# The input projections of the second block as three float32r products of split operands

## The reference

```python
u = rms_norm(h, w_norm_mix[l])
proj = jnp.einsum('btd,dk->btk', u, w_in[l])
conf_a = proj[..., OFF_CONF:OFF_CONF + CONF_WIDTH]
conf_g = proj[..., OFF_CONF + CONF_WIDTH:OFF_Z]
z = proj[..., OFF_Z:OFF_XBC]
xbc = proj[..., OFF_XBC:OFF_DT]
dt_raw = proj[..., OFF_DT:OFF_GATE]
gates = jax.nn.sigmoid(proj[..., OFF_GATE:].astype(jnp.float32)).astype(h.dtype)

c = conf_a * jax.nn.sigmoid(conf_g)
c = depthwise_conv(c, w_conf_dw[l], b_conf_dw[l])
xbc = jax.nn.silu(depthwise_conv(xbc, w_ssm_conv[l], b_ssm_conv[l]))
y = bidir_ssd(xs, dt_raw, ssm_dt_bias[l], ssm_a_log[l], Bs, Cs, ssm_d[l]).reshape(b, Lt, SSM_INNER)
y = rms_norm(y * jax.nn.silu(z), w_ssm_norm[l])
```

## Time and profile before

| what | value |
|---|---|
| median of 3 runs | 2759.58 us |
| lowest, highest | 2759.31, 2762.41 us |
| profiled execution | 2761.74 us |
| its span in the trace | 2760.0 us |
| mean granted TensorE clock | 0.976 |
| scan and what follows it up to the tail | 733 to 1465 us |
| of it the groups 0 to 3 | 797 to 1388 us |
| experts (L1067) | from 1698 us to the end |

### The profile page before, as it was taken

The page is one execution under the profiler, slowest core; times in us unless marked ns, Lnnn a source line. Parts: engine busy times, 40 slices in busy tenths (PEclk is TensorE's granted clock), DMA queues, the critical chain, the costliest instruction groups (busy, mean ns, idle before and its releaser), DMA issues.

```text
span 2760.0 us, 39931 instructions
## 1 busy us (share of the span) xinstructions
PE 2640.1 (96%) x17315; PEld 1608.2 (58%) x17315; DVE 1012.5 (37%) x1458; ACT 673.3 (24%) x1198; POOL 215.7 (8%) x218
## 2 busy tenths in 40 slices
PE   8998899999999999999879997999999999999996
PEld 6754478888787877878669993333333333333332
DVE  4335444433346868685835423111111111111111
ACT  3255433222223333332344222000000000000001
POOL 0022000000002112121200000000000000000000
PEclk9999999999999999999989999999999999999998
DMA  5100022222314142323322246999999999999993
GB/s 203 69 23 1 31 92 92 106 80 97 119 41 140 54 132 62 121 50 92 87 109 82 86 200 244 404 400 407 399 404 394 401 394 398 398 394 391 398 400 135
DMA packets 92619, 560.78 MB, mean 203 GB/s; under 512 B 15236, under 2 KB 48004, under 8 KB 59812
## 3 DMA queue, kind: packets, MB, share of 16 engines
q1 hardware_dynamic: 40320, 514.89, 47.2%
q10 hardware_dynamic: 47236, 30.42, 4.0%
q0 software_dynamic: 4896, 12.98, 1.8%
HBM read 541.97 MB, written 16.29 MB: 202 GB/s over the span
## 4 chain that ended last, share of the span: by engine, by line
PE 90%; DVE 7%; issue 1%; ACT 1%; DMA 0%; POOL 0%; POOLq 0%; ACTq 0%; DVEq 0%; SPq 0%
PE PS L1067 36%; PE PS L509 17%; PE PS L969 5%; PE PS L732 4%; PE PS L728 4%; PE PS L729 4%; PE PS L974 2%; PE PS L703 2%; PE PS L636 2%; DVE H L1878 1%; PE PS L583 1%; PE PS L584 1%; PE PS L587 1%; PE PS L522 1%; PE PS L1057 1%
## 5 line engine op out<-in xcount | busy, mean ns | idle before, releaser
L509 PE MATMUL PS<-U,ring 128*128 128x264 f32 x2304 | 527.4, 389 | 1.3 <-ACT arena L1360 1.3
L1067 PE MATMUL PS<-expert_ring_low,U 128*32 128x512 f32 x4608 | 509.9, 594 | 0.9 <-DVE U L2095 0.9
L1067 PE MATMUL PS<-expert_ring_high,U 128*32 128x512 f32 x4608 | 504.8, 593 | 0.0
L509 PEld LDWEIGHTS PS<-U,ring 128*128 128x128 f32 x2304 | 436.7, 191 | 80.6 <-issue 8.5
L1067 PEld LDWEIGHTS PS<-expert_ring_high,U 128*32 128x32 f32 x4608 | 148.3, 110 | 336.6 <-issue 335.6
L1067 PEld LDWEIGHTS PS<-expert_ring_low,U 128*32 128x32 f32 x4608 | 146.6, 110 | 332.6 <-issue 331.5
L1878 DVE SCALAR_TENSOR_TENSOR H<-arena,par,H 128x528 f32<-128x528 f32 x240 | 188.5, 829 | 1.4
L2107 DVE TENSOR_TENSOR H<-H,PS 128x512 f32<-128x512 f32 x32 | 22.0, 688 | 439.8 <-PE PS L1067 424.3
L728 PE MATMUL PS<-UX,WF 128*128 128x512 f32 x352 | 138.0, 392 | 0.8 <-DVE UX L1639 0.8
L729 PE MATMUL PS<-UX,WF 128*128 128x512 f32 x352 | 137.1, 390 | 0.0
L1290 ACT ACTIVATE WF<-ring 128x1024 fp32r<-128x1024 f32 (+1 forms) x76 | 72.0, 948 | 246.2 <-PE PS L732 245.6
(11 more groups left out here) (327 smaller groups left out, 3214.1 us busy)
## 6 DMA issues: line engine op xcount, KB each, us to landing
expert_ring_low<-w_experts SPq DMA_DIRECT2D x96, 2048.0 KB, 11.3
expert_ring_high<-w_experts SPq DMA_DIRECT2D x96, 2048.0 KB, 11.2
ring<-w_gu SPq DMA_DIRECT2D x11, 2048.0 KB, 7.8
ring<-ssd_sums ACTq DMA_DIRECT2D x32, 512.0 KB, 7.5
ring<-w_xbc SPq DMA_DIRECT2D x8, 1536.0 KB, 6.5
ring<-w_down SPq DMA_DIRECT2D x8, 1408.0 KB, 5.9
ring<-w_in SPq DMA_DIRECT2D x5, 2048.0 KB, 7.9
ring<-w_conf SPq DMA_DIRECT2D x8, 1024.0 KB, 8.6
```

The lines of the kernel that those rows point to most:

```text
L509: last = nc.tensor.matmul(PS[0:M, banks[i], 0:hi - lo], lhs(k), rhs(k)[:, lo:hi], start=(k == 0), stop=(k == K - 1))
L1067: mm = nc.tensor.matmul(PS[QUAD * t:QUAD * t + QUAD, bank, :], stat(t), move(t), start=start, stop=stop)
```

## The change

Each of the 73 projections becomes three float32r products of split operands, as in the tail: weights high x U high, weights high x U low, weights low x U high, 48 matmuls of 264 columns in place of 16 in float32. U is split once, after the normalisation: ScalarE writes the rounded tiles into free space of the ring, VectorE the remainders into `UH`.

Weights now come tile by tile (`w_scan`, 512 KB each) in the order in which PE uses them (`SCAN`), through four places. A tile's load waits until PE has ended the tile four earlier. ScalarE rounds a tile into one of three buffers; it does so directly behind the evacuation of the tile three earlier (`piece_taken`). VectorE subtracts in place (`scan_lows`), at places written into its list. PE waits for the rounded tile ahead of a projection (`fw_high`) and for the remainder ahead of its last 16 matmuls (`fw_low`). The decay arrays move to a slot of their own. The four tail copies into `WH` move behind the last gate tiles on ScalarE, and the loads of `w_co` wait for the last gate tile.

```diff
+SCAN = [("dt",), ("xb", 0, 0), ("xb", 0, 1)] + [(part, u) for u in range(CONF_AHEAD) for part in ("ca", "cg")]
+CHUNK_LAST = {}
+
+
+def _gates(at):
+    SCAN.extend(tag for tag, place in zip(GATE_OF, GATES_AT) if place == at)
+
+
+for _g in range(GROUPS):
+    SCAN += [("xb", _g, _t) for _t in range(6) if _t >= 2 or (_g > 0 and _t == 1)]
+    _gates((_g, "conv"))
+    SCAN += [("zt", 4 * _g), ("zt", 4 * _g + 1)]
+    _gates((_g, "late"))
+    SCAN += [("zt", 4 * _g + 2), ("zt", 4 * _g + 3)]
+    for _c in range(5):
+        _gates((_g, _c))
+        if _g < GROUPS - 1:
+            SCAN.append(("xb", _g + 1, 0) if _c == 4 else (("ca", "cg")[_c % 2], 2 * _g + CONF_AHEAD + _c // 2))
+        CHUNK_LAST[_g, _c] = len(SCAN) - 1
+SCAN += [("g1", m) for m in range(4, DT)]
+SCAN_AT = {tag: n for n, tag in enumerate(SCAN)}
+SRAW, SHIGH = 4, 3
...
+        def scan_place(of, n):
+
+            slot_, at = (RING - 1, max(0, PIECE * n - 512)) if n < SRAW else (0, PIECE * (n % SRAW))
+            width = 64 if n == 0 else P
+            return of[:, slot_, at:at + DT * width].rearrange("p (k n) -> p k n", k=DT)
+
+        def scan_split(n):
+            width = 64 if n == 0 else P
+            at = PIECE * (n % SHIGH)
+            return RF[:, 1, at:at + DT * width].rearrange("p (k n) -> p k n", k=DT)
+
+        def u_high(k):
+            return RF[:, 2, k * T2:k * T2 + T2] if k < DT - 1 else RF[:, 1, PIECE * SHIGH:PIECE * SHIGH + T2]
...
+            def scan_dense(tag, banks, M=P, first=False):
+
+                n = SCAN_AT[tag]
+                open_(tag, *banks)
+                wh, wl = scan_split(n), scan_place(RF, n)
+                pe.wait_ge(S("fw_high"), len(pieces) + n + 1)
+                for k in range(DT):
+                    if first:
+                        pe.wait_ge(S("ux_low"), 2 * DT + k + 1)
+                    for part, x in enumerate((u_high(k), UH[:, k, :])):
+                        for i, (lo, hi) in enumerate(halves(T2)):
+                            nc.tensor.matmul(PS[0:M, banks[i], 0:HT], wh[:, k, :], x[:, lo:hi], start=(k == 0 and part == 0), stop=False)
+                pe.wait_ge(S("fw_low"), len(pieces) + n + 1)
+                for k in range(DT):
+                    for i, (lo, hi) in enumerate(halves(T2)):
+                        last = nc.tensor.matmul(PS[0:M, banks[i], 0:HT], wl[:, k, :], u_high(k)[:, lo:hi], start=False, stop=(k == DT - 1))
+                fill(last, tag)
+
+            scan_dense(("dt",), (6, 7), M=64, first=True)
...
-                dense(tag, (b, b + 1), DT, T2, lambda k: w[:, k, cols], lambda k: U[:, k, :], reads=name)
+                scan_dense(tag, (b, b + 1))
...
+            def scan_highs(upto):
+
+                while scan_next[0] <= min(upto, len(SCAN) - 1):
+                    n = scan_next[0]
+                    act.wait_ge(S(f"ring{scan_ring[n]}"), scan_landed[n])
+                    if n < SHIGH:
+                        got(act, ("dn", DT - 1))
+                    else:
+                        got(act, SCAN[n - SHIGH])
+                    A(scan_split(n), scan_place(ring, n), ACT.Copy).then_inc(S("fw_high"), 1)
+                    scan_next[0] += 1
+
+            def piece_taken(tag):
+                scan_highs(SCAN_AT[tag] + SHIGH)
+
+            scan_highs(1)
             inverse_root("n3", (6, 7), T2)
-
-            got(act, "dt")
-            free(A(tok(DTF[0:64, 1, :], T2), PS[0:64, 6:8, 0:HT], ACT.Identity, bias=par[0:64, PARAMS["dt_bias"]:PARAMS["dt_bias"] + 1]), "dt")
-            act.wait_ge(*freed("dt"))
+            for k in range(DT):
+                act.wait_ge(S("u_ready"), k + 1)
+                A(u_high(k), U[:, k, :], ACT.Copy).then_inc(S("ux_high"), 1)
+            scan_highs(2)
...
                 free(A(tok(CO[:, i % 2, :], T2), PS[:, b:b + 2, 0:HT], ACT.Copy, scale=w), ("xb", g, t))
+                piece_taken(("xb", g, t))
...
                 free(A(tok(SGB[:, :], T2), PS[:, b:b + 2, 0:HT], ACT.Sigmoid), ("cg", u))
+                piece_taken(("cg", u))
...
             root("lnv", (6, 7))
             first_gate(5)
-            got(act, last_read[loads[max(j for j in range(N_DENSE) if slot_of[j] == RING - 1)][0]])
+            squares("ny", lambda k: YT[:, k, :])
+            root("ny", (6, 7), GT[:, 1, :])
+            for m in (6, 7):
+                first_gate(m)
+            act.wait_ge(*freed(("cb", GROUPS - 1, NC - 1)))
...
+            def scan_lows(upto):
+
+                while scan_next[0] <= upto:
+                    n = scan_next[0]
+                    dve.wait_ge(S("fw_high"), len(pieces) + n + 1)
+                    V_.tensor_tensor(scan_place(RF, n), scan_place(ring, n), scan_split(n).bitcast(F32), SUB).then_inc(S("fw_low"), 1)
+                    scan_next[0] += 1
+
+            for k in range(DT + 1):
+                if k < DT:
+                    V_.scalar_tensor_tensor(U[:, k, :], H[:, k, :], pcol("mix_g", k), RS[:, 0:T2], MUL, MUL).then_inc(S("u_ready"), 1)
+                if k == 2:
+                    scan_lows(0)
+                if k >= 1:
+                    dve.wait_ge(S("ux_high"), 2 * DT + k)
+                    V_.tensor_tensor(UH[:, k - 1, :], U[:, k - 1, :], u_high(k - 1).bitcast(F32), SUB).then_inc(S("ux_low"), 1)
+            scan_lows(2)
...
+            scan_lows(SCAN_AT["cg", 1])
             conf_in(0)
...
+                    scan_lows(SCAN_AT["xb", g, 5] - 3 + t)
                     dve.wait_ge(*freed(("xb", g, t)))
...
                 for s, c in enumerate(range(NC - 1, 0, -1)):
                     t0, n = CHUNKS[c]
+                    scan_lows((SCAN_AT["zt", 4 * g + 2] - 1, SCAN_AT["zt", 4 * g + 2], SCAN_AT["zt", 4 * g + 3], SCAN_AT["zt", 4 * g + 3] + 1)[s])
                     got(dve, ("sb", g, c))
...
+                    scan_lows(CHUNK_LAST[g, c])
                     dve.wait_ge(S("e_ready"), i + 1)
...
+            scan_lows(SCAN_AT["g1", 5])
             conf_taps(DT * CONF_TAPS)
...
+            norm_apply("ny", lambda k: YT[:, k, :], lambda k: YT[:, k, :], "y_ready", GT[:, 1, :])
             for p in range(TBUF):
                 tail_split_low(p)
-            norm_apply("ny", lambda k: YT[:, k, :], lambda k: YT[:, k, :], "y_ready", GT[:, 1, :])
...
+                if name == ("co", 0):
+                    for piece in range(len(SCAN)):
+                        if piece == 0:
+                            slot_free(max(j for j in range(n) if slot_of[j] == RING - 1))
+                        elif piece == SRAW - 1:
+                            sp.wait_ge(S("ring2"), scan_landed[piece] - 16)
+                        elif SRAW <= piece < 2 * SRAW:
+                            got(sp, ("dn", DT - 1))
+                            sp.wait_ge(S("fw_high"), len(pieces) + SRAW)
+                        elif piece >= 2 * SRAW:
+                            got(sp, SCAN[piece - SRAW])
+                        src_ = inp["w_dt"][0] if piece == 0 else inp["w_scan"][piece - 1]
+                        sp.dma_start(scan_place(ring, piece).rearrange("p k n -> p (k n)"), src_).then_inc(S(f"ring{scan_ring[piece]}"), 16)
+                    got(sp, ("g1", DT - 1))
```

More of the change, by code:

```diff
@@ L270, in program @@
         SGB = RS
-        FR = [[ring[:, 2 * b + d, 3072:4096].rearrange("p (h n) -> p h n", h=GH) for d in range(2)]
+        FR = [[ring[:, RING - 1, PIECE * (2 * b + d):PIECE * (2 * b + d + 1)].rearrange("p (h n) -> p h n", h=GH) for d in range(2)]
               for b in range(2)]
@@ L359, in program @@
             else:
-                slot_of.append(order_of[turn_ % RING])
-            turn_ += 1
+                slot_of.append(2 + n % 2)
         prev = [max([j for j in range(n) if slot_of[j] == slot_of[n]], default=None) for n in range(len(loads))]
         landed, count = {}, [16, 16, 0, 0]
+        EARLY_RING = [0, 1, 3, 2]
+        scan_ring, scan_landed = [], []
         for n, (name, *_) in enumerate(loads):
+            if name == ("co", 0):
+                for piece in range(len(SCAN)):
+                    i = EARLY_RING[piece] if piece < SRAW else piece % SRAW
+                    count[i] += 16
+                    scan_ring.append(i)
+                    scan_landed.append(count[i])
             count[slot_of[n]] += 16
             landed[name] = count[slot_of[n]]
-        AFTER_FFN = [loads[min(n for n in range(where[("dt",)], N_DENSE) if slot_of[n] == b)][0] for b in (0, 1)]
         last_read = {}
@@ L766, in _ @@
             norm_total("n3", (6, 7), U[:, DT - 1, :], T2)
-            arrived(("dt",))
-            w = slot(("dt",))
-            open_("dt", 6, 7)
-            for k in range(DT):
-                pe.wait_ge(S("u_ready"), k + 1)
-                for i, (lo, hi) in enumerate(halves(T2)):
-                    last = nc.tensor.matmul(PS[0:64, 6 + i, 0:HT], w[:, k, :], U[:, k, lo:hi], start=(k == 0), stop=(k == DT - 1))
-            fill(last, "dt")
-            last_read[("dt",)] = "dt"
+            def scan_dense(tag, banks, M=P, first=False):
```

(18 more changed lines are left out.)

92 lines of the change are left out of this document (27 added, 65 removed).

## The result

| | before | after |
|---|---|---|
| median | 2759.7 us | 2825.5 us (2822.6 to 2830.9, 4 runs) |
| ratio to before, 95% interval | | 1.0239 (1.0221 to 1.0256) |
| span of the profiled execution | 2760.0 us | 2820.9 us |
| mean granted TensorE clock | 0.976 | 0.956 |

What follows compares the result with a forecast made beforehand. PE, busy 96% of the span, was taken as the bound. Front 0, groups +22.6, behind them +2.5 and tail +9.8 gave +35 us; with +18 for the clock on 2759.6, 2812 us, range 2772 to 2850.

Steps and rivals of the forecast that it cites:

- Products 2 to 4: State products after each group's first: VectorE subtracts behind eight taps, then waits about 3.1 us; group 1 +12.6 us, to 43.8.
- The clock: PE's 12 gaps of 4 to 5.3 us may halve its clock: 35 us at worst, half taken, +18.
- The first product: First state product of group 1: VectorE's wait shrinks from 16.33 to 8.2 us, tiles cost 1.2 more; 7 us earlier.
- Chunks: Chunk work of group 1: five subtractions (6.2 us) against shrinking waits for turned outputs, net about -0.1 us.
- Behind the groups: After the last group: two subtractions stand before the last taps, for which PE waits, +2.5 us.
- The tail: Output projection: w_co loads move behind the last gate, so it starts 9.8 us later, with PE idle some 20 us.
- Rival 1: Groups: subtractions fit into VectorE's idle time, 137 us per group for 149, total 2724 us; chance 0.12.
- Rival 2: Groups: tile and decay loads hold ScalarE up, some 10 us in each of four, total 2852 us; chance 0.12.
- Rival 3: Whole kernel: gains and new waits cancel, 2772 us, within 0.2% only if group 0 is free too; chance 0.04.
- shorter than 149 us: Groups of the scan: the prediction called itself wrong if they got shorter than this length.

Runs made afterwards that it cites:

- experiment 1: Changed kernel with four subtractions per group (three in the last) moved ahead of the conformer taps in VectorE's queue, same work: 2773.1 us, 1.0064 of before.
- experiment 2: Changed kernel, same order, with discarded matmuls keeping PE busy ahead of its four waits per group for a subtraction: 2795.5 us, 1.0139 of before.
- experiment 4: Changed kernel with ScalarE's silus and rounded conformer copies ahead of the output-weight copies, VectorE's subtractions likewise: 2814.9 us, 1.0207 of before.
- experiment 8: Changed kernel with subtractions before taps, conformer copies first in the tail, eight taps before the first state product, last taps behind chunk 0's operand: 2731.5 us, 0.9914 of before.

## Why the prediction was right, and where its sizes were off

- **The sign and the mechanism** held. A subtraction queued behind eight taps, PE idle before its last third, and VectorE waiting for the remainder were all forecast, and experiments 1 and 2 confirm them by taking away the order and the clock one at a time.
- **Products 2 to 4**, forecast 43.8 us in group 1, measured 51.0. With the clock held (experiment 2) it is 45.0. The missing 1.2 is about what the first seven taps grew by, beside GpSimd's masks: they took 8.19 us there and 7.83 in the changed kernel, against 6.67 before. The step's arithmetic was right and left out only that.
- **The clock** was taken at half of 35 us. Experiment 2 gives 30. With the clock counted apart, this miss of 12 us is the largest of those that made the forecast too low. The twelve waits took 60.7 us, between 4.7 and 5.6 each, against 3.2 with the clock held, so none of the gaps came and passed in time, as I had let half of them do. The twelve waits make 23 of the 30 us; of the rest, the chunks of groups 0 to 2 hold some 5. The Trainium skill, in "TensorE: Matmul & The Clock Gate", section "HAM oscillation — how this bites in real kernels", says such waits cost anew each time; the trace agrees, and the full 35 of that rule was nearer than the half.
- **The first product** comes 10.6 us earlier than before in group 1, not 7: the wait is 6.71 us instead of 8.2, and the tiles cost 1.0 less, not 1.2 more. They are 6.95 us apart, since a subtraction takes 1.14 in VectorE's stream, not 1.25, and two of them stand just ahead of the first tile and were paid in the chunks.
- **Chunks**, forecast at -0.1 in group 1, took 4.1 more. The waits there could pay back less than I counted: they fell from 7.4 to 2.8 us, while six subtractions cost 6.8, and two of the additions of decay arrays (L2000), beside GpSimd, took 1.93 and 2.07 us instead of 1.22. Experiment 2 says 1.8 of the 4.1 goes with the clock.
- **Behind the groups**: PE's wait ahead of the mean grew by 2.3 us (from 1.12 to 3.38), forecast 2.5. The tail took 8.1 us more, forecast 9.8, and PE stood idle for 19.6 us, forecast some 20. Of these 19.6, 7.1 came back with the order of experiment 4, and the 12.5 that are left there are ScalarE's own silus and copies, not the load.
- **Rival 1** (subtractions fit into idle time, 2724 us) did not occur in the changed order, but its number is close to what VectorE's idle time allowed once used: experiment 8 ends at 2731. **Rival 2** (late loads) did not occur; all subtractions together waited 2.8 us for ScalarE's copies. **Rival 3** was no closer: neither gains nor waits had the sizes it needed.
- The errors partly cancel: the first products gave 13 us more than forecast; products 2 to 4 and the chunks took 40 us more, of which the forecast had 18 as the clock. That the total came within 14 us owes something to luck.
- **Two slips in the prediction.** The 149 us of the earlier trace rows are not a group: by the starts of their convolutions, groups 0 to 2 lasted 139.6, 147.2 and 147.4 us, so "shorter than 149 us" was no test. Changed, they last 160.3 to 160.6. And in group 0 the terms as stated put the first product 2.8 us earlier (16.3 - 8.2 - 7.5 + 2.2), not 3.5; it came 5.2 earlier.

## What to carry over

When an edit makes one engine faster by feeding it from another, look first at the place of the feeding instruction in its queue: four subtractions per group, placed behind eight taps each, cost 52 of the 66 us lost. Price a stall of TensorE at both clock levels, and count the slow level in full if another engine waits for what comes next. And when two engines wait for each other in turn, taking work off one moves the wait; it pays only if the work is put where the other engine is busy.

## What the runs showed of the hardware

- TensorE, idle 4 to 6 us before the last third of a tile, ran it at 0.50 (3.89 us for sixteen matmuls). With up to 44 matmuls of discarded work the clock stayed at 1.00 and the same sixteen took 2.21. Adding work to TensorE made the program 30 us faster.
- A VectorE operation with two SBUF inputs takes 0.76 us alone and 1.54 to 3.95 us beside a busy GpSimd. Moving 15 subtractions of 1.22 us from VectorE to GpSimd, which did them in 2.4, cost 15 us net.
